# Conditioning columns of an adaptive norm: row products on TensorE instead of running sums on VectorE, in a two-layer transformer kernel

## What is computed

```python
def hybrid_layer(x, c, positions, ..., w_ada, b_ada, w_in, ...):
    ada = jax.nn.silu(c) @ w_ada + b_ada              # (1, 1024) @ (1024, 6144)
    shift1, scale1, gate1, shift2, scale2, gate2 = split(ada, 6)
    h = rms_norm(x, norm1_g) * (1 + scale1) + shift1
    proj = h @ w_in                                   # conv, q, k, v, indexer
    ...
    x = x + gate1 * mix                               # mix = [conv, attention] @ w_out
    h2 = rms_norm(x, norm2_g) * (1 + scale2) + shift2
    x = x + gate2 * moe(h2, ...)
```

## Time and profile before

| | |
|---|---|
| Time, median of 3 | 2514.73 us (2512.8 to 2515.73) |
| Span of the profiled execution | 2496.6 us |
| Median less that span | 18.1 us |
| Busy: PE, DVE, ACT | 91%, 63%, 48% |
| First matmul of the input projection | 42.44 us |
| Step 11 begins on VectorE | 136.5 us |
| First attention's fill ends on VectorE | about 256 us |
| Output projection "wout1" | 350 to 391 us |

### The profile page before, as it was taken

The page is one execution under the profiler, slowest core; times in us unless marked ns, Lnnn a source line. Parts: engine busy times, 40 slices in busy tenths (PEclk is TensorE's granted clock), DMA queues, the critical chain, the costliest instruction groups (busy, mean ns, idle before and its releaser), DMA issues.

```text
span 2496.6 us, 31995 instructions
## 1 busy us (share of the span) xinstructions
PE 2274.1 (91%) x10228; PEld 1775.4 (71%) x10228; DVE 1565.3 (63%) x2400; ACT 1194.7 (48%) x1770; POOL 308.4 (12%) x353
## 2 busy tenths in 40 slices
PE   6998999599999999995598989999989878999997
PEld 4776677388777777773475778887868656888875
DVE  6789654599989988986665553332453577333335
ACT  4432433188888888884234333233222573322332
POOL 0000002523333333324300000000020000000000
PEclk8999997799999999997699999999999899999999
DMA  7521132589999999996520122323322101322322
GB/s 308 201 94 59 51 123 104 122 331 390 392 366 380 387 365 366 367 347 236 184 93 9 68 75 94 101 92 101 102 76 92 43 5 64 110 92 101 100 96 82
DMA packets 100027, 422.63 MB, mean 169 GB/s; under 512 B 21025, under 2 KB 21153, under 8 KB 75233
## 3 DMA queue, kind: packets, MB, share of 16 engines
q1 hardware_dynamic: 73600, 367.86, 41.0%
q0 software_dynamic: 25376, 50.66, 5.4%
q10 hardware_dynamic: 960, 2.97, 0.3%
HBM read 419.68 MB, written 39.47 MB: 184 GB/s over the span
## 4 chain that ended last, share of the span: by engine, by line
PE 61%; DMA 14%; DVE 12%; issue 4%; ACT 4%; POOL 2%; DVEq 1%; SPq 0%; ACTq 0%; POOLq 0%
PE PS L284 18%; PE PS L286 17%; PE PS L285 17%; DMA eraw<-wstream 12%; PE PS L637 3%; DVE wl L192 2%; PE PS L659 2%; ACT wh L187 1%; POOL slot_tokens L1696 1%; DVE YA L2323 1%; DMA ada_w<-wada 1%; PE PS L648 1%; DVEq L1203 1%; DVE M L1200 1%; DVE X L563 1%
## 5 line engine op out<-in xcount | busy, mean ns | idle before, releaser
L192 DVE TENSOR_TENSOR wl<-raw,wh 128x1024 fp32r<-128x1024 f32 x239 | 292.6, 1225 | 397.8 <-ACT wh L187 391.4
L284 PE MATMUL PS<-HTh,wh 128*128 128x512 f32 x1248 | 503.3, 403 | 36.0 <-DVE HTl L589 19.4
L192 DVE TENSOR_TENSOR wl<-eraw,wh 128x1024 fp32r<-128x1024 f32 x384 | 460.2, 1225 | 57.1 <-ACT wh L187 56.1
L285 PE MATMUL PS<-HTl,wh 128*128 128x512 f32 x1248 | 491.2, 394 | 0.0
L286 PE MATMUL PS<-HTh,wl 128*128 128x512 f32 x1248 | 490.7, 393 | 0.0
L187 ACT ACTIVATE wh<-raw 128x1024 fp32r<-128x1024 f32 x239 | 251.8, 1056 | 395.2 <-PE PS L286 372.9
L187 ACT ACTIVATE wh<-eraw 128x1024 fp32r<-128x1024 f32 x384 | 395.1, 1054 | 82.0 <-DMA eraw<-wstream 61.0
L284 PEld LDWEIGHTS PS<-HTh,wh 128*128 128x128 f32 x1248 | 237.5, 190 | 102.7 <-issue 36.3
L285 PEld LDWEIGHTS PS<-HTl,wh 128*128 128x128 f32 x1248 | 237.8, 191 | 51.0 <-issue 3.4
L286 PEld LDWEIGHTS PS<-HTh,wl 128*128 128x128 f32 x1248 | 237.4, 190 | 51.0
L284 PE MATMUL PS<-wh,XTh 128*128 128x512 f32 x536 | 223.2, 416 | 3.8 <-DVE XTl L1888 2.4
(11 more groups left out here) (404 smaller groups left out, 3452.9 us busy)
## 6 DMA issues: line engine op xcount, KB each, us to landing
eraw<-wstream SPq DMA_DIRECT2D x192, 1024.0 KB, 14.9
raw<-wstream SPq DMA_DIRECT2D x240, 512.0 KB, 3.3
ada_w<-wada SPq DMA_DIRECT2D x24, 512.0 KB, 4.5
eraw<-wexp SPq DMA_DIRECT2D x9, 1024.0 KB, 8.4
ada_wb<-wada SPq DMA_DIRECT2D x2, 2048.0 KB, 15.9
ada_g<-wada SPq DMA_DIRECT2D x2, 2048.0 KB, 11.0
X<-xT SPq DMA_DIRECT2D x4, 512.0 KB, 8.2
ada_w<-wada SPq DMA_DIRECT2D x1, 2048.0 KB, 23.7
```

The lines of the kernel that those rows point to most:

```text
L192: nc.vector.tensor_tensor(wl[:, ci % RING, :], src, wh[:, ci % RING, :].bitcast(F32), ALU.subtract).then_inc(split_done, 1)
L284: nc.tensor.matmul(o, lh, rh, start=start, stop=False)
L285: nc.tensor.matmul(o, lh, rl, start=False, stop=False)
```

## The change

The 48 columns are made in 12 groups of four, in the order `ADA_GROUPS`: scale1 (two groups), shift1 (two), gate1, scale2, shift2, gate2. For a group n:

- `ada_rows` (TensorE): eight float32 matmuls of 512 columns with 32 columns of stationary data. The moving data is w_ada as it lies; the stationary data is one column of silu(c) copied 32 times (`csilw`). k-tile k writes partitions 32*(k%4) to 32*(k%4)+31 of a PSUM bank, so that four column groups of the array are used and each sums two k-tiles.
- `ada_copy` (ScalarE): 128x512 from PSUM to `ada_row`.
- `ada_columns` (TensorE): four matmuls of one column with the constant `pick` (1 at partitions 0, 32, 64, 96), which add the four partial rows and turn them into columns.
- `ada_add` (VectorE): adds b_ada, 128x4, into `cond`.

`csilb`, its transfer and its activation are gone, and so are the running sums and L960. Rows 0 to 2 stand before the first matmul of the input projection, rows 3 inside `first_pair`, and the others as `ROWS_AT` and `wout_pe` say; columns come one step behind their rows. SyncE's queue has both scale groups, then raw chunks 0 and 1, then the first shift group, then (after `ang`) the second, then raw 2 and 3. Weights of later groups come 2 MB at a time.

```diff
+            ada_a = place("ada_a", [P, 4, CW], 13312)
+            ada_b = place("ada_b", [P, 4, CW], 17408)
             ada_w = place("ada_w", [P, 4, CW], 8192)
+            ada_e = place("ada_e", [P, 3, CW], 5120)
+            ada_f = place("ada_f", [P, 1, CW], 12288)
...
+            ROWS_AT = {1: 4, 2: 5, 4: 6, 11: 7, 12: 8, 13: 9}
...
-                sp.dma_start(ada_wb[:, 0:4, :], wada[0:4].rearrange("c p n -> p c n")).then_inc(shift_in, 16)
-                sp.dma_start(ada_wb[:, 4:8, :], wada[4:8].rearrange("c p n -> p c n")).then_inc(scale_in[0], 16)
...
+                sp.dma_start(ada_a[:], wada[0:4].rearrange("c p n -> p c n")).then_inc(ada_in["a"], 16)
+                sp.dma_start(ada_b[:], wada[4:8].rearrange("c p n -> p c n")).then_inc(ada_in["b"], 16)
                 for c in range(2):
                     sp.dma_start(raw[:, c, :], wstream[c]).then_inc(raw_arrived[c], 16)
+                sp.dma_start(ada_w[:], wada[8:12].rearrange("c p n -> p c n")).then_inc(ada_in["w"], 16)
+                sp.wait_ge(sem("ang"), 1)
+                sp.dma_start(ada_f[:], wada[12:13].rearrange("c p n -> p c n")).then_inc(ada_in["f"], 16)
+                sp.dma_start(ada_e[:], wada[13:16].rearrange("c p n -> p c n")).then_inc(ada_in["e"], 16)
...
-            act.dma_start(csilb[:], cvec).then_inc(sem("c_in"), 16)
...
-                nc.vector.scalar_tensor_tensor(out=w, in0=w, scalar=1.0, in1=csilb[:], op0=ALU.mult, op1=ALU.mult,
-                                               accum_out=adac[:, a:a + 1]).then_inc(ada_used, 1)
...
+            def rows_bank(n):
+                return 5 + n % 2 if n < 10 else n - 8
...
+            def ada_rows(pe, n):
+
+                for name, turn in ADA_IN[n]:
+                    pe.wait_ge(ada_in[name], 16 * turn)
+                if n >= 2:
+                    pe.wait_ge(ada_cond, n - 1)
+                for k in range(DT):
+                    w = ADA_PLACE[n][k // 2][:, k % 2 * 512:k % 2 * 512 + 512]
+                    q = 32 * (k % 4)
+                    mm = nc.tensor.matmul(PS[q:q + 32, rows_bank(n), :], csilw[:, k, :], w, start=k < 4, stop=k >= 4)
+                mm.then_inc(ada_used, 1)
+
+            def ada_copy(act, n):
+                act.wait_ge(ada_used, n + 1)
+                if n >= 2:
+                    act.wait_ge(ada_cols, n - 1 if n < 11 else n)
+                nc.scalar.activation(row_at(n), PS[:, rows_bank(n), :], ACT.Copy).then_inc(ada_copied, 1)
+
+            def ada_columns(pe, n):
+                pe.wait_ge(ada_copied, n + 1)
+                for m in range(4):
+                    mm = nc.tensor.matmul(cols_at(n)[:, m:m + 1], row_at(n)[:, m * P:(m + 1) * P], const("pick"),
+                                          start=True, stop=True)
+                mm.then_inc(ada_cols, 1)
+
+            def ada_add(dve, n):
+                dve.wait_ge(ada_cols, n + 1)
+                a, g = COL_AT["b_ada"][0], 4 * ADA_GROUPS[n]
+                nc.vector.tensor_tensor(cond[:, g:g + 4], cols_at(n), C[:, a + g:a + g + 4], ALU.add).then_inc(ada_cond, 1)
...
                 for m in range(DT):
+                    if m == 3:
+                        ada_copy(act, 3)
+                    act.wait_ge(ada_cond, 3 if m < 4 else 4)
                     act.wait_ge(n_mul, ml0 + m + 1)
...
+                scaled(4)
+                low(2)
+                ada_add(dve, 3)
+                scaled(5)
+                low(3)
...
+                if c in ROWS_AT:
+                    ada_rows(pe, ROWS_AT[c])
+                if c - 1 in ROWS_AT:
+                    ada_columns(pe, ROWS_AT[c - 1])
...
+            def in1_ready(pe, k):
+                if k == 2:
+                    ada_rows(pe, 3)
+                if k == 3:
+                    ada_columns(pe, 3)
+                pe.wait_ge(norm_out, no0 + k + 1)
...
             def wout_pe(pe, c):
+                if c in (3, 4):
+                    ada_rows(pe, c + 7)
+                if c in (4, 5):
+                    ada_columns(pe, c + 6)
                 if c >= 2:
                     x2_sum(pe, c - 2)
```

More of the change, by code:

```diff
@@ L1021, in scaled, with low @@
                                                    op0=ALU.mult, op1=ALU.mult).then_inc(n_mul, 1)
-                scaled(0)
-                split_dve(dve, 0)
-                for m in range(DT):
-                    if m + 1 < DT:
-                        scaled(m + 1)
+                def low(m):
                     dve.wait_ge(n_high, hg0 + m + 1)
@@ L1029, in _ @@
                                                    in1=Hh(m).bitcast(F32), op0=ALU.add, op1=ALU.subtract).then_inc(norm_out, 1)
-                    if m == 0:
-                        split_dve(dve, 1)
+                scaled(0)
+                scaled(1)
+                split_dve(dve, 0)
+                split_dve(dve, 1)
+                scaled(2)
+                ada_add(dve, 2)
+                low(0)
+                scaled(3)
+                low(1)
+                scaled(4)
[3 more added lines that the diff above has]
+                low(3)
+                scaled(6)
+                low(4)
+                scaled(7)
+                for m in range(5, DT):
+                    low(m)
                 split_dve(dve, 2)
@@ L2845, in constants @@
     put("halfpi", np.pi / 2)
+    put("pick", (i % 32 == 0)[:, None])
     return k
```

141 lines of the change are left out of this document (65 added, 76 removed).

## The result

| | before | changed |
|---|---|---|
| median, chip of the prediction | 2514.68 us (4 runs) | 2531.78 us (4 runs) |
| ratio | | 1.0067 [1.0053, 1.0081] |
| profiled execution: span, own time | 2496.6 us, not given | 2531.3, 2533.1 us |
| median, chip of e4_after (below) | 2495.2 us | 2512.2 us |
| ratio there | | 1.0072 [1.0060, 1.0084] |

What follows compares the result with a forecast made beforehand. Bound: transfers and VectorE's sums before 42 us, TensorE to 136, mostly VectorE to about 256, TensorE to 391. Terms -6.5 + 4.65 + 0.7 + 6.75 + 0.1 + 5.9 = +11.6 us gave 2526.3 us, range 2511 to 2540.

Steps and rivals of the forecast that it cites:

- 1, the start: Up to the input projection's first matmul: fewer bytes to wait for, matmul at 35.9 instead of 42.44 us, -6.5 us.
- 2, the first pair: First pair of units: rows 3 and columns 3 come in between, plus a new 1.7 us TensorE wait, +4.65 us.
- 3, behind the pair: Behind the first pair: rows 4 take 2.1 us in a 1.4 us gap of TensorE, +0.7 us.
- 4, steps 2 to 5: Steps 2 to 5: two row products and three turns on TensorE with no gap to take them, +6.75 us.
- 5, steps 11 to 17: Steps 11 to 17: VectorE's 8.2 us relief offset by rows 7 to 9 making its splits wait for TensorE, +0.1 us.
- 6, output projection: Output projection: rows and columns 10 and 11 between units that follow each other without a gap, +5.9 us.
- R: TensorE's time for one group's row product of eight float32 matmuls in four column groups, taken as 2.1 us.
- C: TensorE's time for one group's four one-column matmuls, with a wait before them, taken as 0.85 us (0.8 to 1.0).
- a lower clock behind the new blocks: TensorE behind the added row products: a listed sign that the forecast is wrong, given no size.
- rival (d): Steps 2 to 5: group 5's weights come after 63 us, TensorE idles up to 6 us, 2532 us; 8%.
- Rival (c): Not slower: VectorE gets its 8 us in steps 11 to 17 and the clock stays up, 2511.4 us; 12%.
- The 18.1 us "outside the span": Whole kernel before: the median stands 18.1 us above the profiled span, added to the 2508.2 us span to give 2526.3 us.

Runs made afterwards that it cites:

- e4_after: The changed kernel, unaltered, profiled again on the chip of the first follow-up runs: 2512.2 us, ratio 1.0072 to the kernel before.
- e1_serial: Changed kernel with all eight products of a group in one column group instead of four: ratio 1.0292 to the kernel before.
- e1_two: Changed kernel with two column groups instead of four: +31.6 us to the kernel before, one execution.
- e6_order: Changed kernel with VectorE's add of group 3 moved behind k-tile 3's low part: ratio 1.0050 to the kernel before.
- e3: Changed kernel without row products, copies and columns of groups 4, 5, 6, 10 and 11: 2528.7 us, ratio 1.0130 to the kernel before.
- e2: Changed kernel without row products, copies and columns of groups 7, 8 and 9: ratio 0.9922 to the kernel before.
- e5: Changed kernel with six unread filling products in TensorE's idle places at the start: ratio 1.0048 to the kernel before.
- e7: Changed kernel with gate1, scale2 and gate2 as VectorE's running sums again, shift2's row products behind steps 16 and 18: ratio 1.0048 to the kernel before.
- e9: e7 with group 3's add behind k-tile 3's low part and two filling products: ratio 1.0038 to the kernel before.
- e10: e9 with row products for groups 0 to 3 only, the other groups running sums, 24 of them in steps 2 to 10: 2488.4 us, ratio 0.9972 to before.
- e11: Kernel before with all 24 late running sums in steps 2 to 10 instead of 2 to 17, no row product: 2488.3 us, ratio 0.9969.

## Why the prediction was right, and where it was short

Measured in the first pair of profiles, with the second pair where it differs:

| term | forecast | measured |
|---|---|---|
| 1, the start | -6.5 | -5.9 (-5.7) |
| 2, the first pair | +4.65 | +6.0 (6.4) |
| 3, behind the pair | +0.7 | +1.0 |
| 4, steps 2 to 5 (measured up to step 11) | +6.75 | +6.7 (6.7) |
| 5, steps 11 to 17 | +0.1 | 0.0 |
| fill stage, not in the sum | 0 | +1.9 (-0.4) |
| 6, output projection | +5.9 | +5.9 |
| by the output projection's end | +11.6 | +15.6 (14.0) |

- **The price of a group** was right: R 1.93 us against 2.1, C 0.95 to 1.05 against 0.85. That the two misses cancel is luck: 2.9 us for a group against 2.95. e1_serial and e1_two show that the mechanism is the overlap of groups.
- **Term 1** was right but for its size. The group landed at 28.4 us (28.7 forecast). Product and columns ran wholly at the half level, 3.7 and 1.9 us, where I had taken the middle between the two levels.
- **Term 2 is the term that was mis-sized.** The pair takes 18.8 us instead of 12.75, so 6.0 us more and not 4.65. The new wait was there (1.58 us against 1.7). Missing was the half clock behind it: TensorE went back to that level for 3.4 of the next 3.8 us, which cost 1.6 us. The prediction priced an idle place at its length alone, although a lower clock behind the new blocks stood among its own signs of being wrong. e6_order took the wait and the fall away together, which was worth 2.7 us.
- **Terms 3, 4 and 6** came as worked out; e3 shows that they make up the whole distance to the kernel before. The gap of term 3 was misread: 55.19 us is where ScalarE starts, while TensorE worked on until 55.8 and waited 0.77 us, not 1.4. By that the term would have been +1.3; it is +1.0. TensorE waited for no weights between the first matmul and step 11, so rival (d), whose 2532 us lie nearest to the result, is not what happened.
- **Term 5**, the one against the grain: 8.2 us off the bound engine, gain nothing. Step 11's stretch has the same length to 0.1 us, and e2 gives 7.3 us back when rows 7 to 9 go. The path was as described: from step 11's split to step 15's it took 3.3 us longer than before (3.5 forecast), and the same came back behind it. That the two amounts cancel to nothing is a matter of these sizes. Rival (c), which had VectorE get its 8 us, asked for 4.5 us of TensorE's slack to suffice; it did not.
- **The fill stage's 1.9 us** in the first profile is absent in the second, and TensorE's clock places it. The row from 232 to 244 us in the changed kernel's first profile and in e4_after:

```profile
232.00:244.00 12.00, 11.44 (x31) 7.81 (x32) 8.72 (x29) 4.14 (x15) 0.00 (x0) 0.58 0.19 69
232.00:244.00 12.00, 11.17 (x43) 7.68 (x44) 10.73 (x33) 4.37 (x15) 0.00 (x0) 0.86 0.22 77
```

  In both the level falls behind some 3 us in which TensorE mostly idles; it comes back after 10 us in the one and after 3 in the other, with the same code. From the tenth split to the output projection it takes 112.1 us in e3, e4, e5, e7 and e9, 113.5 in e2, e6 and e10, which have a longer or a further spell at the half level, 114.3 in the first profile of the changed kernel, and 112.4 in the three profiles with the start of before. So two profiles of one kernel differ by 2.2 us here. Whether the change makes such spells more frequent, these profiles don't tell.
- **The 18.1 us "outside the span"** were a wrong reading: 1.8 us lie outside the span, and the rest is an execution that was shorter than the median, for a reason that stays open. It did no harm, since forecast and result are both differences of medians.
- The terms as measured give 13.7 us in the first profiles. The medians are 17.1 us apart; the other 3.4 are the fill stage's 1.9 in that profile, if the executions behind the median have it, and 1.5 which no run places. So part of the miss is outside the sum.

## What to carry to other kernels

Before work moves from the bound engine to another, compare what it adds there with what that engine has in hand at that place. Here some 8 us were added where 4.5 were in hand, and VectorE's relief of 8.2 us came to nothing. Before moving work to another engine, look whether it can be done earlier on the same one: the table of one line in e11 gave the 7.3 us which the row products could not. Price a new idle place on TensorE with the half clock that may follow it (1.6 us behind 1.6 here; nothing behind 0.6 in e5_warm), and never set an add that waits for another engine ahead of work which that engine itself waits for.

## What the runs showed of the hardware

- Four column groups of 32 with float32 operands run side by side almost perfectly: 1.92, 3.64 and 7.05 us for the same sixteen instructions in four, two and one group. Going from whole-array products to column groups and back costs 0.2 us at most.
- TensorE's clock fell to the half level in two settings at the start: at 25.6 to 27.4 us behind 0.9 to 1.1 us of idle time and a block of one-column turns, with more idle time in the changed kernel (the changed kernel, e4_after, e5_warm, e6_order), and at 26.8 us behind 5 us of one-column matmuls without any gap (the kernel before). With turns that take as long (1.94 us) and no idle time ahead of them it stayed full (e1_serial, e1_two).
- It came back at 32.4 us in e5_warm after a block of uninterrupted 512-column products, and at 40.6 us in the changed kernel, 4.1 us into the pair.
- 1.58 us of idle time at 45.6 us were followed by 3.4 us at the half level; 0.6 us at the same place in e5_warm, behind a filling product and a longer stretch at the full level, by none.
- The changed kernel's two profiles differ by 2.2 us in one stage, with such a spell of 10 us in one and of 3 us in the other (fill stage, 0.58 against 0.86 of the clock from 232 to 244 us).
